# The first attention of a two-block kernel: its steps reordered into a finer pipeline

## What is computed

```python
u = rmsnorm(x, g) @ w_in                      # q, k, v, pool and gate columns
a = diff_attention(q, k, v, ...)              # 8 heads, rotary q and k, blocks of 128 queries
#   per head: softmax of two score maps, w = p0 - lam * p1, o = w @ v, rmsnorm of o
p = multiscale_pool(u_pool, w_pool, scale)    # windows 2, 4, 8, 16 by cumulative sums, then a matmul
gates = sigmoid(u_gate)                       # two gates of 1024 columns each
merged = gates[0] * a + gates[1] * p
x = x + merged @ w_out
```

## Time and profile before

| what | us |
|---|---|
| median of 3 runs | 1654.63 |
| the profiled execution, its own time | 1657.15 |
| its span | 1655.4 |
| TensorE matmuls busy in the span | 1605.5 |
| VectorE busy | 929.1 |
| ScalarE busy | 630.2 |
| GpSimd busy | 157.0 |

### The profile page before, as it was taken

How to read it: one execution, slowest core, us unless ns; L and a number is a source line. 1 busy time by engine, 2 the same in 40 slices (tenths; PEclk the granted TensorE clock), 3 DMA queues, 4 the chain that set the end, 5 groups by cost and what they waited for, 6 DMA issues and landing times.

```text
span 1655.4 us, 19077 instructions
## 1 busy us (share of the span) xinstructions
PE 1605.5 (97%) x7352; PEld 1307.0 (79%) x7352; DVE 929.1 (56%) x1364; ACT 630.2 (38%) x1008; POOL 157.0 (9%) x98
## 2 busy tenths in 40 slices
PE   8998989999999999999999999999999999999997
PEld 6776767678888888887777778789888888888886
DVE  6757566655653635345777655556565544444435
ACT  5444645553322212253344434335344323222213
POOL 3001102211000000032222001010001000000002
PEclk9999999999999999999999999999999999999999
DMA  5232322233332333322222133335232323332332
GB/s 195 80 115 68 89 64 80 68 117 100 114 102 90 95 100 98 102 86 85 74 65 64 46 102 96 102 102 166 76 103 77 101 90 102 102 99 93 91 89 76
DMA packets 49674, 155.64 MB, mean 94 GB/s; under 512 B 6192, under 2 KB 9136, under 8 KB 49456
## 3 DMA queue, kind: packets, MB, share of 16 engines
q1 hardware_dynamic: 49584, 154.42, 30.4%
HBM read 148.11 MB, written 2.10 MB: 91 GB/s over the span
## 4 chain that ended last, share of the span: by engine, by line
PE 82%; DVE 10%; ACT 5%; issue 3%; DMA 0%; DVEq 0%; SPq 0%; ACTq 0%
PE G L810 72%; PE SC L810 3%; PE O L810 2%; PE TP L810 2%; DVE WL L1613 1%; PE M L810 1%; DVE T L1836 1%; ACT WH L1205 1%; ACT T L1389 1%; PE TP L1081 1%; ACT L1202 1%; DVE XGl L1614 1%; DVE WTl L1613 1%; DVE T L1824 0%; ACT X L1205 0%
## 5 line engine op out<-in xcount | busy, mean ns | idle before, releaser
L810 PE MATMUL G<-XGh,WH 128*128 128x512 f32 x1248 | 500.8, 401 | 4.5 <-DVE Vl L1614 2.2
L810 PE MATMUL G<-XGh,WL 128*128 128x512 f32 x1248 | 489.7, 392 | 0.0
L810 PE MATMUL G<-XGl,WH 128*128 128x512 f32 x1248 | 489.4, 392 | 0.0
L1613 DVE TENSOR_TENSOR WL<-RAW,WH 128x1024 fp32r<-128x1024 f32 (+3 forms) x253 | 305.3, 1208 | 131.5 <-ACT WH L1205 131.1
L1205 ACT ACTIVATE WH<-RAW 128x1024 fp32r<-128x1024 f32 (+3 forms) x281 | 283.4, 1010 | 178.5 <-PE G L810 168.8
L810 PEld LDWEIGHTS G<-XGh,WH 128*128 128x128 f32 x1248 | 236.3, 189 | 67.0 <-issue 9.2
L810 PEld LDWEIGHTS G<-XGh,WL 128*128 128x128 f32 x1248 | 236.1, 189 | 50.7
L810 PEld LDWEIGHTS G<-XGl,WH 128*128 128x128 f32 x1248 | 236.4, 189 | 47.0 <-issue 0.5
L810 PE MATMUL G<-MGh,WH 128*128 128x512 f32 x412 | 161.8, 393 | 3.6 <-ACT X L1344 2.1
L810 PE MATMUL G<-MGl,WH 128*128 128x512 f32 x412 | 160.7, 390 | 0.2 <-DVE MGl L1613 0.2
L810 PE MATMUL G<-MGh,WL 128*128 128x512 f32 x412 | 160.6, 390 | 0.0
(11 more groups left out here) (305 smaller groups left out, 1879.4 us busy)
## 6 DMA issues: line engine op xcount, KB each, us to landing
RAW<-in_up SPq DMA_DIRECT2D x32, 512.0 KB, 3.6
RAW<-in_dn SPq DMA_DIRECT2D x32, 512.0 KB, 3.6
RAW<-in_fg SPq DMA_DIRECT2D x22, 512.0 KB, 3.5
RAW<-in_fu SPq DMA_DIRECT2D x22, 512.0 KB, 3.6
RAW<-in_g SPq DMA_DIRECT2D x16, 512.0 KB, 3.6
RAW<-in_f SPq DMA_DIRECT2D x16, 512.0 KB, 3.6
X<-in_x SPq DMA_DIRECT2D x16, 256.0 KB, 4.7
RAW<-in_q SPq DMA_DIRECT2D x8, 512.0 KB, 3.6
```

Source lines behind the costliest of these rows:

```text
L810: return e.matmul(dst, st, mv, start=start, stop=stop, skip_group_check=True)
L1613: return e.tensor_tensor(dst, src, hi.bitcast(F32), ALU.subtract)
```

## The change

The sequence of the arithmetic on each value stays; the list of steps is cut finer and laid out anew.

1. **Steps split at their hops between engines.** scores_a gives its exp to a step exp_a one tick later; weights_a moves to two ticks after the scores, turn_a to four, its split (wt_a) to five. pv_a, its square (sq_a), the sum of squares with Ln and Exp (ss_a, rs_a) and the scaling (op_a) come at ticks 6, 7, 8, 8 and 9. The rotary embedding becomes seven steps in a tick each (two a tick for the first pair).
2. **Chains.** Window sums (win), the pooling difference (diff, diff_hi, diff_lo) and the merges (mix_y; mix_o, sum_a, sum_hi, sum_lo) are put in chains; each tick emits one of their steps, two if more than `BACKLOG` are left. `until` emits ticks with no matmul unit between them until a needed step is out.
3. **Gates in two buffers**: the first gate of odd heads goes to RB; the gated pooled value is written over the pooled one.
4. **Weights**: the splits of g0 and g1 leave GpSimd for VectorE; for q, k, pool, g0, g1 the third unit ahead is split before the second half of a unit, not before the first.
5. **Order and pace**: four q/k pairs come first, attention starts at place 4 of a new `HEADS_A`, `PACE_A` 1.75; wp comes later. Evacuations of G (qk, gate, pool_in) are emitted behind the tick's attention steps.

```diff
-ON_POOL = ("g0", "g1", "qb", "kb", "ub")
+ON_POOL = ("qb", "kb", "ub")
...
-FIRST_A, PACE_A = 5, 1.8
+FIRST_A, PACE_A, BACKLOG = 4, 1.75, 6
+STAGES_A = (("exp_a", 1), ("weights_a", 2), ("turn_a", 4), ("wt_a", 5))
+CLOSING_A = (("pv_a", 6), ("sq_a", 7), ("ss_a", 8), ("rs_a", 8), ("op_a", 9))
...
+    def one_of_chains(self):
+        if self.chains:
+            steps = self.chains.pop(0)
+            self.put(*steps.pop(0))
+            if steps:
+                self.chains.append(steps)
...
+    def until(self, *step):
+        while step not in self.emitted and not any(step in steps for steps in self.chains):
+            self.tick()
...
         g = self.bank(step)
         self.tick()
-        u = self.unit_of[step] = self.take(name, i)
+        wide = self.units[self.taken][2] > S
+        late = wide and name in ("q", "k", "pool", "g0", "g1")
+        u = self.unit_of[step] = self.take(name, i, NW - 1 if late else NW)
         self.put("mm", u, g, 0)
         self.tick()
-        if self.units[u][2] > S:
+        if wide:
+            while self.split < min(u + NW, len(self.units)):
+                self.split_one()
             self.put("mm", u, g, 1)
...
             elif kind == "gate":
+                if i > 0:
+                    self.until("mix_y", i - 1)
                 for w in range(2):
+                    if i > 1:
+                        self.until("sum_lo", i - 2)
                     self.gemm(("g0", "g1")[w], i, ("gate", i, w))
-                    self.put("gate", i, w)
+                    self.later(0, "gate", i, w)
...
-                self.unit_of["wp", i] = self.take("wp", i)
+                self.until("diff_lo", i)
+                if i > 0:
+                    self.until("sum_a", 2 * i - 1)
+                self.tick()
+                while any(("ss_a", h) in self.emitted and ("rs_a", h) not in self.emitted for h in range(8)):
+                    self.tick()
+                self.unit_of["wp", i] = self.take("wp", i, NW - 1)
                 self.bank(("wp", i))
                 self.put("wp", i)
+                self.later(0, "wp_out", i, first=True)
...
         def gate_of(h, w):
-            return X[:, 2 + w, :]
+            return X[:, 3, :] if w == 1 else (X[:, 2, :], RB[:, :])[h % 2]
```

More of the change, by code:

```diff
@@ L111, in __init__, with chain @@
         self.taken, self.split, self.loaded = 0, 0, 0
+        self.chains, self.emitted = [], set()
         self.build()
     def put(self, *step):
+        assert step[0] != "diff_hi" or step[1] == 0 or ("wp", step[1] - 1) in self.emitted
         self.steps.append(step)
+        self.emitted.add(step)
+    def chain(self, n, *steps):
+        self.later(n, "chain", list(steps))
+    def one_of_chains(self):
[7 more added lines that the diff above has]
+            self.tick()
+        for steps in self.chains:
+            while step in steps:
+                self.put(*steps.pop(0))
+        self.chains = [steps for steps in self.chains if steps]
+        assert step in self.emitted, step
     def later(self, n, *step, first=False):
@@ L123, in tick @@
         for step in self.jobs.pop(self.clock - 1, ()):
-            self.put(*step)
+            if step[0] == "chain":
+                self.chains.append(step[1])
+            else:
+                self.put(*step)
+        self.one_of_chains()
+        if sum(len(steps) for steps in self.chains) > BACKLOG:
+            self.one_of_chains()
     def drain(self):
-        while self.jobs:
+        while self.jobs or self.chains:
             self.tick()
@@ L255, in heads_a @@
                 gated[i] = self.clock
-                if i in done and (i < 4 or i % 2 == 1):
-                    self.merge_a(i, max(done[i] + 1, self.clock))
+                if ("wp", i // 2) in self.emitted:
+                    self.chain(1, ("mix_y", i))
+                    self.merge_a(i, max(done[i] + 1, self.clock + 2))
             elif kind == "pool":
+                if i > 0:
+                    self.until("diff_lo", i - 1)
                 self.gemm("pool", i, ("pool_in", i))
-                self.put("pool_in", i)
@@ L261, in heads_a @@
-                self.later(1, "pool_diff", i)
-            else:
-                self.unit_of["wp", i] = self.take("wp", i)
+                self.later(0, "pool_in", i)
+                self.chain(1, *(("win", i, j) for j in range(i + 1)), ("diff", i), ("diff_hi", i), ("diff_lo", i))
+            else:
+                self.until("diff_lo", i)
+                if i > 0:
+                    self.until("sum_a", 2 * i - 1)
[3 more added lines that the diff above has]
+                self.unit_of["wp", i] = self.take("wp", i, NW - 1)
@@ L673, in program @@
         win_step, pd_hi, pd_lo = sem("win_step"), sem("pd_hi"), sem("pd_lo")
[L674 removed]
+        PDH, PDL = tally("diff_hi"), tally("diff_lo")
         WIN_END, n = {}, 0
```

196 lines of the change are left out of this document (111 added, 85 removed).

## The result

The changed kernel took **1639.78 us** (median of 4 runs, 1636.55 to 1640.54) against 1654.72 us for the kernel before in the same session: ratio 0.9903, 95% interval 0.9886 to 0.9921. The gain is 14.9 us where 16.6 were forecast. The profiled execution was the fastest of the four, and the profiled one of before lay 2.5 us above its median, so the spans differ by more, 20.6 us.

A forecast was written before the change was run, and what follows sets the result against it. TensorE's waits for late engines, and slow clock behind them, were taken as the bound in the first attention. Of 29.7 us, 3.6 + 6.6 + 1.4 + 1.5 = 13.1 stay and 16.6 go: 1638 us, range 1626 to 1652.

The forecast's parts named there:

- What can be won: First attention: TensorE's 21.8 us of standing still plus 8.5 us of slow clock, 30.3 us, of which 29.7 can go.
- Halves to VectorE: 16 gate weight halves add 18 us to VectorE, less stretching gives back 14; busy about 195 us (177 to 210), not the bound.
- rival A: VectorE's long pieces have another cause than GpSimd: 18 us added, none given back; gain 8, 1646 us; chance 0.13.
- The shorter ticks: Exp, window sums and rotation as separate steps: no cost outside the bursts; about 1 us each if cover goes.
- The three Ln places: Heads 1, 4, 5, where Ln and Exp meet a weight split: TensorE waits 1.2 us each, 3.6 us (0 to 12.0).
- The burst at wp1: After k7, wp1, sum of squares and two score products without a unit between: 4.9 us waiting, 1.7 us slow clock.
- The slow clock: TensorE's lower clock behind waits over 2 us: five stretches cost 8.5 us before; 1.7 us stays, behind wp1.
- The other bursts: Steps without a unit between: wp2 1.0 us, wp3 0.4, wp0 and g1 of 5 nothing; each at most 6.6.
- Rival D: Slower: all five bursts wait as wp1 does, 38 us against 29.7, 8 us more, 1663 us; chance 0.11.
- B: Rival: everything covered, only a burst of 2 us remains, 1625 to 1628 us; chance 0.08.
- C: Rival: the same waits elsewhere, 12 + 6.6 + 10 + 1.5 = 30, no difference, 1652 to 1657 us; chance 0.11.
- Waits added and moved: Gates waiting for merges, rotary DMAs and later splits in the first attention cost nothing; unplaced small waits 1.5 us (0 to 5).

The follow-up runs named there:

- after_exp0: The changed kernel with the exp again in the tick of its score product, as in the kernel before: 1651.06 us, ratio 0.9983.
- after_held: The changed kernel with a weight split that would follow Ln and Exp in the same tick put off until the next take: 1631.28 us, ratio 0.9864.
- before_exp: The kernel before with each score product one tick earlier, its exp left in place as a step of its own: 1656.15 us, ratio 1.0013.
- after_early: The changed kernel with after_held's edit, wp1 before q7 and k7, and the pooling difference's last step before the second gate unit ahead of a wp: 1632.34 us.
- after_gate: The changed kernel with the first gate no longer waiting in the list for mix_y of the head before: 1638.19 us, ratio 0.9902.

## Why the prediction was right, point by point

The mechanism holds: waits and the slow clock behind them are what went, and what is left stands where the sum had it. That the number came within 1.7 us owes something to luck. Between the two profiled executions the gain is 20.6 us, 4 more than forecast, and between the medians 1.7 less; the forecast took what one execution could win, 2.5 us above its median, off the median as well.

*What can be won.* 30.3 us was too little. The stage lost 19.3 us, and waits and clock of some 15 us are left, together 34. The idle column counts from a matmul's modelled end; from start to start each wait is some 0.16 us longer (4.19 us of idle time is 4.35 us late). Counted so, the sixteen waits of over 0.4 us in the kernel before make 24.2 us against the 21.8 of the windows. That gives 2.4 of the missing 3.7 us; the rest I can't place.

*Halves to VectorE.* VectorE 190.3 us, forecast 195 (177 to 210). The 18 us added were about right, 19.1 measured; the 14 given back were 20. That it would not be the bound held. That the edit brings nothing in the new list was in the sum, which had no term for it. What rival A charged for the stretches, some 9 us, no run shows: none has the halves on VectorE and the stretches too.

*The shorter ticks.* Costed at nothing outside the bursts, and no wait of TensorE over 0.3 us stands in them. after_exp0 shows that this paragraph carried the result: one of its ticks is worth 13 us in the new list, more than I gave any single edit. The prediction named the exp in half a sentence and did not price what stands behind it in ScalarE's queue.

*The three Ln places.* Forecast 1.2 us each, 3.6 together; 1.60, 1.27 and 1.30 late, 4.2 together. The chain is the one shown, and after_held removed it by one of its links.

*The burst at wp1.* Forecast 4.9 us in two waits; 0.78 and 4.18 us of idle time, 4.96. Counted as late it is 0.95 + 0.31 (the two matmuls of the sum of squares) and 4.39, 5.65. The table load took 1.28 us and Ln began 0.01 us behind its end (229.29). The Trainium skill ("ScalarE: Activation LUTs", What ACT_TABLE_LOAD costs) adds a drain of about 1.38 us; the trace does not agree, and with it the chain would have been that much longer. The sum was right to go by the earlier trace rows.

*The slow clock.* This is the term that was mis-sized. I took 1.7 us behind wp1 and none behind a wait under 2 us. The two stretches of clock 0.51 behind wp1 reach from 232.5 to 239.4; from the score product on, 5.3 us ran at half speed, 2.6 us lost. And three of five executions show the slow clock behind the 1.6 us wait of head 1. The mean granted clock of the runs puts a size on it: 0.990 in the median of the kernel before beside the experiments, 0.9925 and 0.9935 in the runs of the changed one. That is some 16 us of lost clock over the whole program against 11 to 12, so 4 to 6 us came back where the sum had 6.8 (8.5 less 1.7), an estimate, and a third decimal is 1.6 us. Without it the medians are 10 to 11 us apart, which is the gain in waits; the sum had 9.8. So the missing 1.7 us are clock, as far as these figures reach.

*The other bursts.* wp2 1.0 forecast, 0.80 + 0.41 late. wp3 0.4 forecast, 0.99 late. wp0 and g1 of 5 nothing, as forecast. Rival D had them all at wp1's price and is out, and so are B and C by the time. C's sum does not come out as written: other bursts at 4 us each are 8 us for two or 16 for four, not 10.

*Waits added and moved.* No wait of TensorE for a weight half or a rotary DMA stands between 60 and 346 us. before_exp shows how little the rotation has to spare in the old list: one tick less, and TensorE stands for 8 us.

## What to carry to other kernels

Where engines walk one list in order, look for each instruction that is queued in the tick of its producer: it holds its whole queue for as long as the producer takes, and what stands behind it pays. Within the new list one tick of distance was worth 13 of 15 us, while moving 19 us of work between engines was worth nothing there. Made alone in the old list the tick brought nothing, where it also ran into a wait of 8 us for a DMA, and the move brought about 4 us: what an edit is worth depends on the list around it. Once the waits are few, taking away one often moves the others: price a wait by what is late next, and try the edit that takes one link out of a chain (after_held, 22 us under the kernel before) ahead of those that shift the list.

## What the runs showed of the hardware that was not expected

**Slow clock behind short waits, and not in every execution.** I took the granted clock over the 5 us behind each wait of the first attention, in all fourteen profiles. Behind all 17 waits that made TensorE 3.0 us late or more it was 0.66 or lower, and so it was behind 11 of the 13 between 2.0 and 2.8 us. The same wait of 1.6 us, at the same place in five executions, has it in three; behind ten others between 1.6 and 1.9 us late there is none (in two of these cases it comes only with the next, longer wait). The plainest case stands just ahead of the first attention, in a part that no kernel here changes: near 57 us a matmul that waits for a low half from VectorE is 2.35 us late in every one of the fourteen profiles. In seven the slow clock follows, in seven it does not. The windows behind it in after_held and in after_early (columns as in the earlier trace rows):

```profile
57.65:62.65 5.00, 5.00 (x15) 3.97 (x16) 3.05 (x4) 0.68 (x1) 0.00 (x0) 0.66 0.40 134
```
```profile
57.42:62.42 5.00, 5.00 (x22) 4.15 (x23) 3.05 (x4) 0.67 (x1) 0.00 (x0) 1.00 0.43 138
```

So a wait between 1.6 and 2.5 us late has no fixed price, and two executions of one kernel can differ by some us with identical waits. The six runs of after_gate show the most: 1635.0 us at a mean granted clock of 0.996, 1642.5 us at 0.990. Such stretches also come in the second block, which no kernel here edits: the profile of before shows two there, at 768 and 956 us, at which matmuls start 0.43 us apart for 3 us, that of after one, at 936. That is a part, 1.7 us, of the difference between the 20.6 us of the two profiled executions and the 15 of the medians.

**A stretched VectorE that costs nothing.** In the new list L1919 over 512 columns takes 1308 ns in the mean beside GpSimd's pieces and 751 without, and the kernel's time is the same. Here the busy time of an engine said little, and the order of its queue at the waits said much.
